# Two transformer blocks in one kernel: another order of the work at the borders between stages

## The chip, the cores and the metric

The kernel runs on one core of one Trainium2 chip. The time is the device time of one execution in microseconds; the number given for a kernel is the median of its runs. TensorE (PE in the profile) multiplies, VectorE (DVE) and ScalarE (ACT) do the elementwise work, GpSimd (POOL) makes constants, SyncE (SP) issues all DMAs.

## The reference

Everything is float32, on 256 tokens of width 2048. Two blocks follow each other.

```python
# first block, two layers
h = rmsnorm(x, norm_g[l]); proj = h @ w_in[l]            # 6 x conv, 4 groups of diff, 2 of mem
y_a = short_gated_conv(a_x, a_b, a_c, conv_w[l], conv_b[l]) * silu(a_g)
y_d = diff_attention(rmsnorm(q), rmsnorm(k), v, lam, slopes) (normed) * silu(d_g)   # 6 heads
mkv = rmsnorm(mem, mem_norm_g[l]) @ w_mem_kv[l]
y_m = memory_attention(rmsnorm(mq), rmsnorm(mk), mv) * silu(m_g)                    # 4 heads
x = x + concat(y_a, y_d, y_m) @ w_out[l]
# second block, one layer; mod = silu(c) @ w_mod + b_mod gives sh1, sc1, g1, sh2, sc2, g2
h = rms(x) * (1 + sc1) + sh1; proj = h @ w_in_2
o_a = sliding_window_attention(rope(q_a), rope(k_a), v_a, sinks)
o_b = rms(gla_chunked(q_b, k_b, v_b, gk), gla_norm) * silu(og_b)
merged = sigmoid(g_a) * (o_a @ w_br_a) + sigmoid(g_b) * (o_b @ w_br_b)
x = x + g1 * rms(merged @ w_out_2)
x = x + g2 * rms(conv_ffn(rms(x) * (1 + sc2) + sh2))
```

## The kernel before

**Precision and units.** Each product is computed from parts: an activation tile and a weight tile are each split into a high part (rounded to fp32r) and a low part (the rest). The activations stand in `XH[:, tile, 0:512]`, high in the first 256 columns and low in the others, for 16 tiles of the contraction. A *unit* is 512 KB of weights, four contraction tiles by two output tiles. It lands by DMA in one of five RAW buffers, ACT rounds it to `WH` (`act_split`, L540), DVE subtracts to get `WL` (`dve_split`, L549), and PE multiplies: `WH` with 512 columns (L468), `WL` with 256 (L473), 16 matmuls a unit. `WH` and `WL` are rings of four, so at unit w the engines split unit w+4 (`split_ahead`, L555), and ACT's split waits until PE is done with unit w. Semaphore `unit_done` counts PE's units, `split_ready` DVE's splits.

**Stages.** A stage is one matrix (mem0, mem1, qkv0, heads0a to heads0c, out0, and so on), its pairs of output tiles take `per_pair` units each, usually four. A turn is `body` pairs. After the units of a pair ACT copies the part of the bank that came from the low activations to `HIGH` (L804) and DVE adds the two and finishes (`evacuate`, L938 to L961). In token stages (v_b, out1, mix_out and the down stages) the tokens are on the partitions of the output and a pair is 512 output columns for both halves of the tokens; their unit, two contraction tiles by four output tiles, is 12 matmuls (L415 to L417).

**Order of the work.** All instruction streams are written out by hand and each engine runs its own in order. In `act_stage` and `dve_stage` a turn goes over b and q: the split for four units ahead, then whatever is attached to this place (squares, sums, attention steps `act_beside`, `dve_beside`, one step of the modulation product `dve_modulation`, L1932), then after the pair the evacuation. PE has attached work too, in `pe_stage`, and waits in order for what it needs. SP issues the loads of units and modulation steps in one order (`program_sync`); each waits until the buffer five loads back is used.

**Borders.** The next stage's input is split chunk by chunk, four tiles each (`act_input_chunk`, L1121 and L1127; `dve_input_chunk`, L1138 and L1146). `input_waits` (L1106) holds a chunk until its source is ready and until the old stage no longer reads those tiles of XH. `then` and `inside` (L239 to L247) say how many chunks are placed in the last pair of the old stage; the rest follow its last evacuation.

Around the change:

- mem0 to mem1: the four chunks of mem1's input are in mem0's last pair. In the same turn ACT squares x for its norm (`act_squares`, L1094, at w 3 and 4) and DVE adds them up (`dve_presum`, L1076 and L1078, at w 5 and 6); PE sums them over partitions in mem1 after unit 1 (`presummed_sums`, L1084).
- heads0c and heads1c (`beside="mem"`) carry two turns of memory attention: at w 2 scores, w 3 exps, w 5 transposes (L1247) and their copy by ACT (`act_copy_turned`, L1307), w 6 values (L1268), w 7 output. In turn 0 ACT also makes the Silu of the gates M_G (4 tiles) and D_G (6 tiles) at w 4 (L1411 to L1415). In the third turn the branches are finished: Silu of A_G, products, chunks 0 to 2. Chunk 3 follows the last evacuation (`act_mix_end`, `dve_mix_end`), then a table load.
- out0 ends with x1's chunks 0 to 2 inside and chunk 3 behind, branch_b with those of m.
- g_b's input is all 16 tiles of XH; branch_a's (oa) has 8 tiles, placed at 0 to 7; branch_b's (ob) has 16: chunks 0 and 1 in branch_a's last pair, 2 and 3 behind it.

## Time and profile before

| what | value |
|---|---|
| runs | 2597.15, 2598.98, 2601.71 us, median 2598.98 |
| profiled execution, span | 2596.0 us (its own device time is not given apart from the span) |
| PE busy | 98% |
| DVE busy | 75% |
| ACT busy | 50% |
| DMA | 556.64 MB, 214 GB/s |
| mean granted TensorE clock | 0.995 |

The span goes from the first to the last instruction. Units follow each other on PE at an even pace, so a border is read by its excess over whole units. PEclk in a window is the granted clock as a share of 2.4 GHz; 0.50 is 1.2 GHz. In a timeline the first number is the start, the second the time until the end of the group, and the bracket tells for how long the engine was idle before and what released it.

### The profile page before, as it was taken

Reading aid. Unit: us, or ns where it says so; the run is one execution under the profiler, and the core shown is the slowest. Engines: PE = TensorE matmul, PEld = TensorE weight load, DVE = VectorE, ACT = ScalarE, POOL = GpSimd, SP = SyncE. Lnnn points to the kernel's source line nnn. Section 1 sums busy time; section 2 is a strip of 40 time slices with the busy share of each in tenths; the row PEclk is TensorE's granted clock in tenths of the full one; section 3 lists DMA queues with packets and bytes.
Section 4 is the critical chain, followed back from the end, with each engine's and each line's share of the span. In section 5 each row is a group of like instructions: output and inputs, shape, how many; then the busy total and the mean of one; then the engine's idle time right before and its main releaser. Section 6 shows DMA issues by size and latency. Waiting matters only on the chain.

```text
span 2596.0 us, 35319 instructions
## 1 busy us (share of the span) xinstructions
PE 2547.3 (98%) x13936; PEld 2175.1 (84%) x13936; DVE 1939.5 (75%) x2769; ACT 1300.1 (50%) x1758; POOL 10.8 (0%) x62
## 2 busy tenths in 40 slices
PE   7999999999999999999999999999999999999998
PEld 6888888888888887888788888888888888888886
DVE  6877766887777687676667787887788887788855
ACT  7544555554455555454444554544644443444443
POOL 0000000000000010000000000000000000000000
PEclk9999999999999999999999999999999999999999
DMA  8687554778754466755567788888476668976764
GB/s 271 219 299 244 160 154 143 228 258 286 242 158 152 149 214 218 235 171 154 153 190 222 231 277 277 270 282 272 143 197 189 188 208 307 284 203 196 201 194 140
DMA packets 526519, 556.64 MB, mean 214 GB/s; under 512 B 17409, under 2 KB 453762, under 8 KB 526226
## 3 DMA queue, kind: packets, MB, share of 16 engines
q1 hardware_dynamic: 526354, 554.38, 68.4%
q8 instruction: 110, 1.80, 0.3%
q14 instruction: 55, 0.45, 0.1%
HBM read 552.22 MB, written 2.10 MB: 214 GB/s over the span
## 4 chain that ended last, share of the span: by engine, by line
PE 88%; DVE 7%; ACT 3%; issue 1%; DMA 0%; DVEq 0%; SPq 0%; ACTq 0%
PE ACC L468 43%; PE ACC L473 21%; PE ACC L415 6%; PE ACC L417 6%; PE ACC L416 6%; DVE WL L549 2%; PE OU L1268 1%; ACT WH L540 1%; PE SC L1235 1%; PE SC L1247 1%; ACT PROB L1293 1%; PE SC L1276 1%; DVE XH L1138 0%; DVE XH L1146 0%; DVE PROB L1352 0%
## 5 line engine op out<-in xcount | busy, mean ns | idle before, releaser
L468 PE MATMUL ACC<-XH,WH 128*128 128x512 f32 x5296 | 1692.3, 401 | 21.2 <-DVE XH L1146 15.3
L540 ACT ACTIVATE WH<-RAW 128x1024 fp32r<-128x1024 f32 (+1 forms) x852 | 897.9, 1057 | 1166.5 <-PE ACC L473 836.1
L549 DVE TENSOR_TENSOR WL<-RAW,WH 128x1024 fp32r<-128x1024 f32 (+1 forms) x852 | 1032.6, 1220 | 568.5 <-ACT WH L540 567.0
L473 PEld LDWEIGHTS ACC<-XH,WL 128*128 128x128 f32 x5296 | 998.7, 189 | 236.6
L473 PE MATMUL ACC<-XH,WL 128*128 128x256 f32 x5296 | 1044.2, 279 | 0.0
L468 PEld LDWEIGHTS ACC<-XH,WH 128*128 128x128 f32 x5296 | 814.4, 189 | 41.2 <-issue 18.5
L1932 DVE SCALAR_TENSOR_TENSOR RAWMOD<-RAWMOD,CSILU 128x1024 f32<-128x1024 f32 x192 | 233.8, 1218 | 1.0 <-DMA RAWMOD<-in_w_mod_t 0.7
L415 PE MATMUL ACC<-WH,XH 128*128 128x512 f32 x384 | 151.9, 396 | 3.6 <-DVE WL L549 3.6
L416 PE MATMUL ACC<-WL,XH 128*128 128x512 f32 x384 | 149.6, 390 | 0.0
L417 PE MATMUL ACC<-WH,XH 128*128 128x512 f32 x384 | 149.5, 389 | 0.0
L415 PE MATMUL ACC<-WH,AH 128*128 128x512 f32 x352 | 137.3, 390 | 0.0
L417 PE MATMUL ACC<-WH,AH 128*128 128x512 f32 x352 | 137.0, 389 | 0.0
L416 PE MATMUL ACC<-WL,AH 128*128 128x512 f32 x352 | 137.0, 389 | 0.0
L415 PEld LDWEIGHTS ACC<-WH,XH 128*128 128x128 f32 x384 | 72.1, 188 | 22.1 <-issue 7.5
L804 ACT ACTIVATE HIGH<-ACC 128x512 f32<-128x512 f32 (+1 forms) x171 | 89.9, 526 | 0.0
L417 PEld LDWEIGHTS ACC<-WH,XH 128*128 128x128 f32 x384 | 72.1, 188 | 15.3
L416 PEld LDWEIGHTS ACC<-WL,XH 128*128 128x128 f32 x384 | 72.1, 188 | 14.4
L417 PEld LDWEIGHTS ACC<-WH,AH 128*128 128x128 f32 x352 | 66.1, 188 | 13.8
L416 PEld LDWEIGHTS ACC<-WL,AH 128*128 128x128 f32 x352 | 66.1, 188 | 13.5
L415 PEld LDWEIGHTS ACC<-WH,AH 128*128 128x128 f32 x352 | 66.1, 188 | 13.5
L938 DVE TENSOR_TENSOR PR<-ACC,HIGH 128x512 f32<-128x512 f32 x64 | 43.7, 682 | 3.6 <-ACT HIGH L804 3.6
L979 DVE SCALAR_TENSOR_TENSOR CV<-U,PARAM,CV 128x256 f32<-128x256 f32 x88 | 42.7, 485 | 3.1
(287 smaller groups left out, 1438.0 us busy)
## 6 DMA issues: line engine op xcount, KB each, us to landing
RAW<-in_w_in SPq DMA_DIRECT2D x408, 512.0 KB, 4.5
RAWMOD<-in_w_mod_t SPq DMA_DIRECT2D x192, 512.0 KB, 4.9
RAW<-in_w_up SPq DMA_DIRECT2D x176, 512.0 KB, 4.7
RAW<-in_w_out SPq DMA_DIRECT2D x96, 512.0 KB, 5.4
RAW<-in_w_down SPq DMA_DIRECT2D x88, 512.0 KB, 5.0
RAW<-in_w_mem_kv SPq DMA_DIRECT2D x32, 512.0 KB, 5.8
RAW<-in_w_branch_gla SPq DMA_DIRECT2D x32, 512.0 KB, 5.1
RAW<-in_w_branch_attn SPq DMA_DIRECT2D x16, 512.0 KB, 5.2
```

The lines of the kernel that those rows point to most:

```text
L415: pe.matmul(bank, x, high[:, kc], start=tile == 0, stop=False)
L416: pe.matmul(bank, x, low[:, kc], start=False, stop=False)
L417: mm = pe.matmul(bank, operand[:, tile, T + b * P:T + b * P + P], high[:, kc], start=False, stop=tile == WK * stage.per_pair - 1)
L468: return pe.matmul(bank, k.WH[:, w % RING, kc, cols], x, start=tile == 0, stop=False)
L473: return pe.matmul(bank[:, 0:T], k.WL[:, w % RING, kc, cols], x[:, 0:T], start=False, stop=tile == tiles - 1)
L540: act.activation(k.WH[:, slot, :, 0:width], k.RAW[:, r % RAWS, :, 0:width], ACT.Copy).then_inc(k.hi_ready, 1)
L549: dve.tensor_tensor(k.WL[:, slot, :, 0:width], k.RAW[:, k.plan.unit_load[unit] % RAWS, :, 0:width], k.WH[:, slot, :, 0:width].bitcast(F32) ...
L804: act.activation(k.HIGH[:, first:stage.tiles], k.ACC[:, bank + first:bank + stage.tiles, T:2 * T], ACT.Copy).then_inc(k.high_ready, 1)
L938: chain.link(dve.tensor_tensor(dst, low, high, ALU.add))
L979: dve.scalar_tensor_tensor(out=cv, in0=u[:, 0:T], scalar=column(taps[0]), in1=cv, op0=ALU.mult, op1=ALU.add).then_inc(done, 1)
L1235: mm = pe.matmul(k.SC[:, c, b * T:b * T + T], q, keys, start=True, stop=True)
L1932: dve.scalar_tensor_tensor(out=raw, in0=raw, scalar=1.0, in1=k.CSILU[:, half * MOD_COLS:(half + 1) * MOD_COLS], op0=ALU.mult, op1=ALU.mult ...
```

## The change

1. `evacuates_first` for heads0c, heads1c, out0 and branch_b: in the last pair the split for four units ahead and the modulation step of the last unit stand behind the evacuation, on ACT and DVE.
2. In heads0c and heads1c, turn 0: Silu of M_G right after the copy of the turned probabilities at w 5, Silu of D_G and the table load at w 6.
3. The squares of x move from mem0's last turn (w 3, 4) to mem1's first (w 1, 2), their presums to w 2 and 3, PE's sums and ACT's rstd from after unit 1 to after unit 4 of mem1, the memory keys from 3 to 6, on DVE from 4 to 7.
4. Table loads ahead of out0, out1, mix_out and down1 are left out; loads of the same set stand later in out0 (w 6), mix_out and down1 (second pair, q 1).
5. g_b goes over its k tiles in the order 2, 3, 0, 1 (`MIXED`), with the rows of the weights to match; branch_a's input is placed in XH tiles 8 to 15 and read there; ob's chunks 0 and 1 go into tiles 0 to 7 inside branch_a (turns 1 and 2, w 1), chunks 2 and 3 into its last pair.

Left out below: the new attributes of `Stage` (`ahead`, `order`, `evacuates_first`) and the field `place` of `Prep` (0; for oa 2 * UK), which is added to f in both input chunk functions.

```diff
...
@@ -122,6 +123,13 @@
     view = w.rearrange("(k p) n -> p k n", p=P)
     return lambda j, q: view[:, UK * q:UK * q + UK, bass.ds(first + 2 * P * j, width)]
+
+
+def mixed_columns(w, first):
+
+    view = w.rearrange("(k p) n -> p k n", p=P)
+    return lambda j, q: view[:, UK * MIXED[q]:UK * MIXED[q] + UK,
+                             first + 2 * P * j:first + 2 * P * j + 2 * P]
@@ -215,7 +223,7 @@
     s.append(Stage("og", columns(w, 5648), 4, 8, 4, h2, "plain", OG, beside="gla", first=0))
     s.append(Stage("g_a", columns(w, 7696), 4, 8, 4, h2, "plain", G_A, beside="gla", first=2))
-    s.append(Stage("g_b", columns(w, 9744), 4, 8, 2, h2, "plain", G_B))
+    s.append(Stage("g_b", mixed_columns(w, 9744), 4, 8, 2, h2, "plain", G_B))
     oa_in = split_input(2)
     s.append(Stage("branch_a", columns(d["w_branch_attn_2"][0], 0), 2, 8, 2, oa_in, "times", G_A))
@@ -241,6 +249,10 @@
         by_name[name].then, by_name[name].inside = then, inside
     by_name["qkv1"].sums_last = 2
+    by_name["branch_a"].ahead = 2
+    by_name["g_b"].order, by_name["branch_a"].order = MIXED, MIXED
+    for name in ("heads0c", "heads1c", "out0", "branch_b"):
+        by_name[name].evacuates_first = True
     for l in range(DEPTH):
         by_name[f"heads{l}c"].inside = 3
@@ -459,6 +471,8 @@
         else:
             s, tile, tiles = h, UK * q + kc, UK * stage.per_pair
+            return (k.ACC[:, bank0 + s], operand[:, UK * stage.order[q] + kc], s, tile, tiles, kc,
+                    slice(h * P, h * P + P))
         return (k.ACC[:, bank0 + s], operand[:, tile], s, tile, tiles, kc,
                 slice(h * P, h * P + P))
@@ -505,11 +519,11 @@
                     for c in range(4):
                         presummed_sums(pe, k, 0, c)
-                if stage.name == "mem1" and (i, w) == (0, 1):
+                if stage.name == "mem1" and (i, w) == (0, 4):
                     pe.wait_ge(k.rstd_ready, 1)
                     for c in range(4):
                         presummed_sums(pe, k, 1, c)
-                if stage.name == "mem1" and (i, w) == (0, 3):
+                if stage.name == "mem1" and (i, w) == (0, 6):
                     pe_memory_keys(pe, k, 0)
                 if stage.name == "qkv0" and (i, w) == (0, 5):
@@ -552,6 +566,11 @@
 
 
+def at_end(stage, last, b, q):
+
+    return stage.evacuates_first and last and b == stage.body - 1 and q == stage.per_pair - 1
+
+
 def split_ahead(engine, k, stage, i, w, last, split):
@@ -572,6 +591,8 @@
             if stage.name == "out1" and (j, q) == (2, 5):
                 act_rotary(act, k)
+            if stage.name in ("mix_out", "down1") and (j, q) == (1, 1):
+                act.preload_act_table_set("natural_log_exp_and_others")
             if stage.name == "down1" and j == 0 and q in (2, 4, 6, 8):
                 act_gain_rows(act, k, 1, q // 2 - 1)
@@ -758,7 +779,8 @@
         for b in range(stage.body):
             for q in range(stage.per_pair):
-                split_ahead(act, k, stage, i, b * stage.per_pair + q, last, act_split)
+                if not at_end(stage, last, b, q):
+                    split_ahead(act, k, stage, i, b * stage.per_pair + q, last, act_split)
                 act_beside(act, k, stage, i, b * stage.per_pair + q, chain)
                 if stage.kind == "ffn":
@@ -774,13 +796,13 @@
                 if stage.name == "mem0" and (i, w) == (1, 2):
                     act_small(act, k)
-                if stage.name == "mem0" and i == 1 and w in (3, 4):
+                if stage.name == "mem1" and i == 0 and w in (1, 2):
                     act.wait_ge(k.x_landed, 64)
-                    for c in (2 * w - 6, 2 * w - 5):
+                    for c in (2 * w - 2, 2 * w - 1):
                         act_squares(act, k, 1, c)
-                if stage.name == "mem1" and (i, w) == (0, 1):
+                if stage.name == "mem1" and (i, w) == (0, 4):
                     act_rstd(act, k, 1, chain)
-                if stage.name == "mem1" and (i, w) == (0, 3):
+                if stage.name == "mem1" and (i, w) == (0, 6):
                     act_memory_keys(act, k, 0, chain)
                 if stage.sums_last is not None and w == 3 and i == 0:
@@ -794,8 +816,12 @@
                 if stage.name == "g_b" and w == 6:
                     act_gain_rows(act, k, 0, i)
+                if stage.name == "branch_a" and w == 1 and i in (1, 2):
+                    act_input_chunk(act, k, k.preps["ob"], i - 1)
+                if stage.name == "out0" and (i, w) == (0, 6):
+                    act.preload_act_table_set("natural_log_exp_and_others")
                 if last and b == stage.body - 1 and q < stage.inside and stage.then:
-                    act_input_chunk(act, k, k.preps[stage.then], q)
+                    act_input_chunk(act, k, k.preps[stage.then], q + stage.ahead)
             bank = 2 * ((stage.pair0 + b) % 2)
             first = 1 if stage.kind == "ffn" else 0
@@ -804,10 +830,12 @@
                            k.ACC[:, bank + first:bank + stage.tiles, T:2 * T],
                            ACT.Copy).then_inc(k.high_ready, 1)
+            if at_end(stage, last, b, stage.per_pair - 1):
+                split_ahead(act, k, stage, i, stage.units - 1, last, act_split)
 
     stage_turns(stage, turn)
     if stage.then is not None:
-        for c in range(stage.inside, k.preps[stage.then].chunks):
+        for c in range(stage.inside + stage.ahead, k.preps[stage.then].chunks):
             act_input_chunk(act, k, k.preps[stage.then], c)
     if stage.norm is not None:
@@ -1003,7 +1031,8 @@
             for q in range(stage.per_pair):
                 w = b * stage.per_pair + q
-                split_ahead(dve, k, stage, i, w, last, dve_split)
+                if not at_end(stage, last, b, q):
+                    split_ahead(dve, k, stage, i, w, last, dve_split)
                 if stage.kind == "ffn" and q == 2:
                     gate(i, b)
@@ -1014,26 +1043,36 @@
                     dve_modulation_sums(dve, k, k.plan.mod_adds[unit], chain)
                 dve_beside(dve, k, stage, i, w, chain)
-                if stage.name == "mem0" and (i == 0 and w in (1, 2) or i == 1 and w in (5, 6)):
-                    for c in (2 * (w - 4 * i) - 2, 2 * (w - 4 * i) - 1):
-                        dve_presum(dve, k, i, c, chain)
+                if stage.name == "mem0" and i == 0 and w in (1, 2):
+                    for c in (2 * w - 2, 2 * w - 1):
+                        dve_presum(dve, k, 0, c, chain)
+                if stage.name == "mem1" and i == 0 and w in (2, 3):
+                    for c in (2 * w - 4, 2 * w - 3):
+                        dve_presum(dve, k, 1, c, chain)
                 if stage.name == "mem0" and (i, w) == (0, 6):
                     dve_lambdas(dve, k, chain)
-                if stage.name == "mem1" and (i, w) == (0, 4):
+                if stage.name == "mem1" and (i, w) == (0, 7):
                     dve_memory_keys(dve, k, 0)
                 if stage.name == "qkv0" and (i, w) == (0, 6):
                 if stage.name == "kv_a":
                     dve_decays(dve, k, w)
-                for n in k.plan.mod_steps.get(unit, ()):
+                if not at_end(stage, last, b, q):
+                    for n in k.plan.mod_steps.get(unit, ()):
+                        dve_modulation(dve, k, n)
+                if stage.name == "branch_a" and w == 1 and i in (1, 2):
+                    dve_input_chunk(dve, k, k.preps["ob"], i - 1)
+                if last and b == stage.body - 1 and q < stage.inside and stage.then:
+                    dve_input_chunk(dve, k, k.preps[stage.then], q + stage.ahead)
+            evacuate(i, b)
+            if at_end(stage, last, b, stage.per_pair - 1):
+                split_ahead(dve, k, stage, i, stage.units - 1, last, dve_split)
+                for n in k.plan.mod_steps.get(end_unit(stage) - 1, ()):
                     dve_modulation(dve, k, n)
-                if last and b == stage.body - 1 and q < stage.inside and stage.then:
-                    dve_input_chunk(dve, k, k.preps[stage.then], q)
-            evacuate(i, b)
 
     stage_turns(stage, turn)
     if stage.then is not None:
-        for c in range(stage.inside, k.preps[stage.then].chunks):
+        for c in range(stage.inside + stage.ahead, k.preps[stage.then].chunks):
             dve_input_chunk(dve, k, k.preps[stage.then], c)
@@ -1108,15 +1147,20 @@
         wait_from_zero(engine, sem, value)
     if prep.free is not None:
-        early = prep.free.per_pair - c - 1 if c < prep.free.inside else 0
-        engine.wait_ge(k.unit_done, end_unit(prep.free) - early)
+        stage = prep.free
+        if c < stage.ahead:
+            engine.wait_ge(k.unit_done, stage.unit0)
+            return
+        inside = c - stage.ahead
+        early = stage.per_pair - inside - 1 if inside < stage.inside else 0
+        engine.wait_ge(k.unit_done, end_unit(stage) - early)
 
 
     input_waits(act, k, prep, c)
     if prep.gain is None:
-        f = 4 * c
+        f = 4 * c + prep.place
         for first, count in prep.chunk(c):
             last = act.activation(k.XH[:, f:f + count, 0:T], k.PR[:, first:first + count, :],
...
@@ -1204,7 +1249,7 @@
         "y1": prep(plan.y_in[1], "heads1c", mixed_ready(1), chunk=mixed),
         "oa": prep(plan.oa_in, "g_b", lambda k, c: [(k.unit_out, units_of(2) + 8)], chunks=2,
-                   chunk=tiles(O_A)),
+                   chunk=tiles(O_A), place=2 * UK),
         "ob": prep(plan.ob_in, "branch_a", lambda k, c: [(k.gated, 1)], chunk=tiles(V_B)),
         "m": prep(plan.m_in, "branch_b", pairs_of("branch_b"), chunk=tiles(G_A)),
@@ -1408,15 +1453,16 @@
     elif w == 1 and kind == "win" and stage.first + i == 0:
         act_decay_logs(act, k)
-    elif w == 4 and kind == "mem" and i == 0:
-        act.wait_ge(k.evacuated, stage.pair0)
-        act_silu(act, k, M_G, MEM_T)
-        act_silu(act, k, D_G, DIFF_T)
-        act.preload_act_table_set("natural_log_exp_and_others")
     elif w == (4 if kind == "win" else 3):
         act_exps(act, k, kind, u, sinks=2 * (stage.first + i) if kind == "win" else None)
     elif w == (6 if kind == "win" else 5):
         act_copy_turned(act, k, kind, u)
+        if kind == "mem" and i == 0:
+            act.wait_ge(k.evacuated, stage.pair0)
+            act_silu(act, k, M_G, MEM_T)
+    elif w == 6 and kind == "mem" and i == 0:
+        act_silu(act, k, D_G, DIFF_T)
+        act.preload_act_table_set("natural_log_exp_and_others")
     elif w == 6 and kind == "mem" and i == 1:
         act_conv_centre(act, k, stage.layer)
@@ -2125,7 +2171,6 @@
             products(name.format(l))
         act_mix_end(act, k, l)
-        tables()
         products(f"out{l}")
     act_token_norm(act, k, s["out1"], chain)
@@ -2137,12 +2182,10 @@
     products("branch_a")
     products("branch_b")
-    tables()
     products("mix_out")
     act_token_norm(act, k, s["mix_out"], chain)
     for name in ("up0", "down0", "up1"):
         products(name)
-    tables()
     products("down1")
```

## Rows read from the trace of the kernel before

**Rows 1.** the page, part 1: busy us of each engine, share of the span, instructions

```profile
PE 2547.3 (98%) x13936; PEld 2175.1 (84%) x13936; DVE 1939.5 (75%) x2769; ACT 1300.1 (50%) x1758; POOL 10.8 (0%) x62
```

**Rows 2.** PE's waits: engine line waited for: us in total, times, longest

```profile
PE OU L1268 <- ACT TURNED L1307: 4.5, 2, 2.3
```

**Rows 3.** windows: stretch, us, busy us (instructions) by engine, PEclk, DMA share, GB/s

```profile
650.83:664.77 13.94, 13.94 (x83) 12.16 (x82) 10.85 (x14) 6.27 (x7) 0.00 (x0) 1.00 0.83 260
950.62:972.38 21.76, 21.76 (x97) 18.02 (x96) 15.78 (x20) 10.62 (x13) 0.00 (x0) 1.00 0.90 298
57.02:72.39 15.37, 11.97 (x59) 10.01 (x57) 13.34 (x25) 12.90 (x24) 0.00 (x0) 0.89 0.30 105
27.43:31.76 4.33, 4.33 (x27) 3.79 (x25) 3.32 (x6) 1.06 (x1) 0.00 (x0) 1.00 1.10 347
409.72:421.31 11.59, 9.33 (x43) 7.69 (x42) 3.07 (x3) 6.16 (x6) 0.00 (x0) 0.85 0.45 137
441.97:449.36 7.39, 7.39 (x43) 6.47 (x42) 6.34 (x7) 5.46 (x9) 0.00 (x0) 1.00 0.54 156
477.23:481.97 4.74, 2.95 (x18) 2.39 (x16) 2.74 (x5) 3.13 (x5) 0.00 (x0) 1.00 0.38 121
936.72:942.38 5.66, 2.88 (x14) 2.10 (x12) 3.36 (x5) 4.90 (x6) 0.00 (x0) 1.00 0.16 61
569.78:581.13 11.35, 8.94 (x42) 7.55 (x41) 9.28 (x15) 6.28 (x9) 0.00 (x0) 0.85 0.58 186
1657.35:1665.36 8.01, 5.99 (x35) 4.91 (x33) 7.98 (x11) 7.47 (x9) 0.00 (x0) 1.00 0.82 272
1760.04:1763.71 3.67, 2.88 (x13) 2.10 (x12) 2.47 (x4) 3.66 (x4) 0.00 (x0) 1.00 0.24 88
```

**Rows 4.** timeline of ACT before out1: start us, us, engine line op tiles [idle before]

```profile
938.62 1.28 ACT L2115 ACT_TABLE_LOAD   x1
939.92 1.06 ACT L540 ACTIVATE WH<-RAW 128x1024 fp32r<-128x1024 f32 x1
```

**Rows 5.** timeline of ACT in mem0's last pair

```profile
52.89 2.00 ACT L1094 ACTIVATE PR<-X 128x1024 f32<-128x1024 f32 x2
```

**Rows 6.** timeline of DVE from mem0's last pair into mem1

```profile
53.01 1.23 DVE L549 TENSOR_TENSOR WL<-RAW,WH 128x1024 fp32r<-128x1024 f32 x1 [4.56 <-ACT WH L540]
...
62.56 0.69 DVE L1076 TENSOR_TENSOR PR<-PR 128x512 f32<-128x512 f32 x1
...
64.68 1.66 DVE L1146 SCALAR_TENSOR_TENSOR XH<-Y,PARAM,XH 128x256 fp32r<-128x256 f32 x4
...
66.26 1.22 DVE L549 TENSOR_TENSOR WL<-RAW,WH 128x1024 fp32r<-128x1024 f32 x1
...
73.83 0.68 DVE L938 TENSOR_TENSOR PR<-ACC,HIGH 128x512 f32<-128x512 f32 x1
...
76.67 2.35 DVE L549 TENSOR_TENSOR WL<-RAW,WH 128x1024 fp32r<-128x1024 f32 x2
...
78.94 1.22 DVE L1932 SCALAR_TENSOR_TENSOR RAWMOD<-RAWMOD,CSILU 128x1024 f32<-128x1024 f32 x1
```

**Rows 7.** timeline of DVE at the end of heads0c

```profile
476.61 0.68 DVE L938 TENSOR_TENSOR PR<-ACC,HIGH 128x512 f32<-128x512 f32 x1
...
477.33 0.69 DVE L940 TENSOR_TENSOR PR<-PR,RSTD 128x512 f32<-128x512 f32 x1
...
478.72 0.69 DVE L1577 TENSOR_TENSOR PR<-PR 128x512 f32<-128x512 f32 x1 [0.70 <-ACT PR L1508]
...
480.63 1.29 DVE L1138 TENSOR_TENSOR XH<-PR,XH 128x512 fp32r<-128x512 f32 x2 [1.22 <-ACT XH L1121]
```

**Rows 8.** timeline of DVE at the start of out1

```profile
941.01 2.36 DVE L549 TENSOR_TENSOR WL<-RAW,WH 128x1024 fp32r<-128x1024 f32 x2 [1.07 <-ACT WH L540]
```

**Rows 9.** timeline of DVE at the end of out0

```profile
570.23 0.69 DVE L950 TENSOR_TENSOR SUM<-ACC,HIGH 128x512 f32<-128x512 f32 x1
...
573.42 1.67 DVE L1146 SCALAR_TENSOR_TENSOR XH<-X,PARAM,XH 128x256 fp32r<-128x256 f32 x4 [1.77 <-ACT XH L1127]
```

12 lines of the change are left out of this document (7 added, 5 removed).

## The prediction

> **What bounds the kernel now.** I read the page first: TensorE (PE) is busy for 2547.3 of the 2596.0 us of the span [rows 1], so this change can give back only what PE waits. The list of PE's waits comes next, for what it waits for: of the waits touched here it names one pair, the value matmuls for ACT's copy into TURNED, 4.5 us in two times [rows 2]; the others are waits for DVE at stage borders. Then the windows. In an undisturbed stretch five units of 16 matmuls take 13.94 us, 2.79 us each, and eight units of a token stage take 21.76 us, 2.72 each [rows 3]. Against these two numbers every window at a border shows its loss directly; the reader should subtract whole units and look at PEclk, the granted clock. Where it is under 1.00, part of the window ran at 1.2 GHz instead of 2.4. Last, the timelines of DVE and ACT at the borders, to see what their queues hold.
>
> The losses that the edits touch, all from [rows 3]:
> - mem0 to mem1, 57.02 to 72.39: three units and the four sums. Three units are 8.36, the sums cost 4.33 - 2.79 = 1.54, so the loss is 15.37 - 9.90 = 5.47. It is two waits and a stretch at the low clock (0.89).
> - heads0c, 409.72 to 421.31: 11.59, where the same two units of the next turn take 7.39 at full clock: 4.20. It comes twice, once in each layer (two waits in [rows 2]): 8.4.
> - heads0c to out0: 4.74 - 2.79 = 1.95. heads1c to out1: 5.66 - 2.72 = 2.94.
> - out0 to qkv1, 569.78 to 581.13: 11.35 less two units (5.58) and sums (1.54): 4.23. The mean clock of 0.85 says that 0.15 x 11.35 = 1.7 of it is missing clock, the price of one fall; the wait is the other 2.5.
> - branch_a to branch_b: 8.01 - 5.58 = 2.43. branch_b to mix_out: 3.67 - 2.72 = 0.95.
>
> Together 26.4 us, about 1% of the time. No edit can bring more.
>
> **Silu of the memory gates.** Today ACT runs both Silus and two table loads between the exps and the copy of the turned probabilities, and PE's value matmuls wait for the copy [rows 2]. In the new order the copy comes right after PE's transposes, within the 2.79 us of the unit that PE runs in between. What moves behind it is a table load (1.28, [rows 4]), the Silu of M_G's four tiles, a split, the Silu of D_G's six and a second load: 1.0, 1.06 and 1.5 for the three in between, at 1.0 for each four tiles as in the squares [rows 5] and 1.06 for the split [rows 4], some 6 us in all. PE needs none of it: the only PE work behind ACT is a split used three units, 8.4 us, later, and DVE needs M_G after the value matmuls. Both losses should go with their low clock: **-8.4**. If that cover failed, PE would wait again at the same place for up to the same time; bounds 0 and -8.4. I take the full value, since the turn behind it, which has no Silu, shows 7.39 [rows 3].
>
> The table load takes 1.28 us in the trace, and ACT's next instruction starts 1.30 after it began [rows 4]. The Trainium skill (ScalarE: Activation LUTs, What ACT_TABLE_LOAD costs) adds a drain of about 1.38 us to each switch. By that the block would be 2.8 us longer, still inside the 8.4 us, so the sum would stay, while the chance of the second rival below would double.
>
> **mem0 to mem1.** The squares of x leave ACT ahead of the chunks of mem1's input: two groups of 2.00 [rows 5]. ACT then has chunk 0 ready about 3.8 us earlier, and every DVE low part comes before PE wants it. The loss of 5.47 goes. But the work comes back in mem1. PE now does the sums of x after unit 4 of mem1 and needs all four presums there. PE arrives at 57.02 + 6 x 2.79 = 73.75. DVE is in order and, from its split at 53.01 on (the row shows the idle 4.56 before it), has without a hole: nine splits at 1.135 (half of 78.94 - 76.67; 10.2), one evacuation (1.34, as two operations in [rows 7]), four input chunks at 1.58 (6.3), the block of the last evacuation, small gains and key squares (76.67 - 73.83 = 2.84), one modulation step (1.15), and two pairs of presums at 2.12 (4.24) [rows 6]. That is 26.1, so the last presum ends near 79.1. It stands behind split 7 of mem1, and PE, also in order, waits for it, 5.4 us nearly idle, with its units 5 and up queued behind the sums. Three quarters of the 1.54 for the sums pass in that time, so unit 5 starts at 79.65 instead of 75.29: 4.36 lost. In the trace such long waits were followed by half clock; with one fall at 1.7 that is **+6.1**. Net: -5.47 + 6.06 = **+0.6**. Bounds of the new wait: 0, if DVE were early, and 8.5, if the modulation step's transfer comes 2.5 late as well. I keep the queue's own sum since each term has a row. Behind PE's wait ACT's rstd waits too, and with it splits 9 on; these are needed three units later and PE is stopped anyway. The sums of the memory keys, two units later, wait for nothing new.
>
> **Evacuation ahead of the split.** At heads0c's end DVE's last evacuation starts one split (1.14) earlier than 476.61. Silu and the gate product follow, but the split now stands between evacuation and product: it ends 1.34 + 1.135 after the new start of 475.47, at 477.94, against 478.72 today. So 0.79 of the 1.14 stays, the low part of chunk 3 starts at 479.84 instead of 480.63 [rows 7], and PE too: **-0.8** of 1.95; 1.2 stay. Bounds 0 and -1.95.
>
> heads1c to out1 is the same chain (the same 0.8), but the wait is for the first split behind it, and the table load falls out: ACT's split comes 0.8 + 1.3 earlier, at 937.8. DVE is free for it only after chunk 3's low part, which today starts as the table load does: 938.62 - 0.8 + 1.3 = 939.1, against 941.0 today: **-1.9** of 2.94 [rows 3, 4, 8]. Bounds -0.8 and -2.9.
>
> At out0's end a split and a modulation step stand ahead of the evacuation, which starts at 570.23. It now goes first and they follow, all three ending at the old 571.57; chunk 3's high part is done on ACT by then, so the low part starts at 571.57, not 573.42 [rows 9]: -1.85, leaving a wait of 0.7. Waits of that size stand in the trace at full clock (0.95 at mix_out, [rows 3]), so the fall goes as well: **-3.55**. Bounds -1.1 and -4.2.
>
> branch_b to mix_out: the same edit with three evacuation steps, and a table load out of ACT's way. The first split behind the border comes over 2 us earlier, the wait was 0.95: **-0.95**. Here and at the other borders the last split (2 us later) frees its RAW buffer later, and SP's in-order queue holds the next loads; these have units to spare, since the first split that is late for PE today gets earlier. The moved preloads fall into ACT's idle time, nothing on PE's path.
>
> **Branches.** ob's chunks 0 and 1 are split inside branch_a into the half of XH that g_b has left, 2.1 us of ACT and 2.3 of DVE over two turns with slack. Chunks 2 and 3 are then where 0 and 1 were, wanted two units later: **-2.43**. g_b's other k order costs nothing: same bytes, same matmuls. Bounds -2.43 and +0.5 (a late split, if DVE's 7.98 busy of 8.01 at the border spread backwards).
>
> **Sum.** -8.4 + 0.6 - 0.8 - 1.9 - 3.55 - 0.95 - 2.43 = -17.4 us. The span of 2596.0 would be 2578.6. Of the profiled execution only its span is given; the median of the runs, 2598.98, lies 3.0 above it (2597.15 to 2601.71). With the same 3.0 around it: **2581.6 us**.
>
> **Rivals.**
> - *The presums are in time*: PE finds them, or DVE works ahead. For it: in the trace DVE does catch up within a turn. Against: no hole in its queue. Then 6.1 less: 2575.5. Chance 0.12.
> - *The Silu wait only changes its name*: DVE's output or a late split holds PE in the same unit. Against: 8.4 us of cover. Then +8.4: 2590.0. Chance 0.04.
> - *DVE's order gives nothing at the three borders with little slack* (out0, out1, qkv1), since the split that is put back takes what the evacuation gains; this is also the case that the change does not do there what it says. +0.8 + 1.9 + 1.85: 2586.2, or 2587.9 if the clock falls there too. For it: a third of the gain is lost so already at out0. Chance 0.12.
> - *Slower*: the long wait in mem1 brings the clock down and it stays down. Place: from 74 us on; price: the same 1.7 for each stretch like that after out0. It decides from 11 such stretches in a row (17.4 / 1.7 = 10.2); with 14 it is 2605.4. Against: after every wait of this trace the clock was back within one or two. Chance 0.03.
>
> **How the numbers follow.** My forecast has 0.63, its own range 2577.5 to 2585.5: one fall of the clock more or less at out1's end or in mem1 (1.7 each way) and 2 us for the border estimates. The rest, 0.06, is mixtures. The range 2574.5 to 2588.5 takes in the first and third rival and leaves out the others. A measurement here tells 0.2%, 5.2 us, from no change. Faster than 2593.8: 0.94; within: 0.04; slower: 0.02.
>
> **What would show it.** In the new trace: the value matmuls (L1268) out of PE's waits; no wait at the start of mem1, but one of about 5 us for DVE's presum at 74 us, with half clock behind it; waits of 1.2, 1.1 and 0.7 at out0, out1 and qkv1; none at branch_b and mix_out. I am wrong if the sums do not wait, if a border waits for a DMA, or if the clock falls at a wait of about 1 us.

## The result, and the profile after

The kernel after takes 2582.76 us (median of 4 runs, 2582.33 to 2582.91), beside 2600.35 us of the kernel before (4 runs, 2597.15 to 2602.24). The ratio is 0.9933, 95% interval 0.992 to 0.9947: 17.6 us less. The forecast was 2581.6, a step of -17.4. The span goes from 2596.0 to 2580.6 us. Repeated later beside 8 new runs of before (median 2598.73, 2596.86 to 2604.61), after took 2582.0 (5 runs, 2581.32 to 2583.65).

Page, part 1, of the kernel after: PE's busy time moves by only 3.6 us (2547.3 to 2543.7), with the same matmuls. The other 11.8 of the span's 15.4 are waiting.

```profile
PE 2543.7 (99%) x13936; PEld 2172.3 (84%) x13936; DVE 1939.0 (75%) x2769; ACT 1297.0 (50%) x1756; POOL 10.8 (0%) x62
```

PE's waits in the kernel after (waiting instruction, awaited instruction: us in total, times, longest). The value matmuls' wait for TURNED of [rows 2] is out of the list. L1117, the presum, is new, and so is L981, an evacuation in branch_a. The presum's 3.0 come in three pieces, since PE does each sum as soon as its presum is there.

```profile
PE OU L1123 <- DVE PR L1117: 3.0, 3, 1.5
...
PE ACC L482 <- DVE XH L1182: 1.0, 1, 1.0
PE ACC L482 <- DVE PR L981: 1.0, 2, 0.5
PE ACC L427 <- DVE WL L563: 0.8, 1, 0.8
```

Windows of the kernel after, from a unit's first matmul to another's (stretch, us, busy us of PE, PEld, DVE, ACT, POOL, PEclk, DMA share, GB/s). In order: mem0's last unit to mem1's third; mem1 units 4 and 5 with the sums; heads0c; out0's third unit; qkv1; heads1c; out1; kv_a's first three units; branch_a units 6 to 11; branch_a to branch_b; mix_out. They answer to the windows of [rows 3], except the second, the eighth and the ninth, which lie elsewhere.

```profile
56.43:64.79 8.36, 8.36 (x51) 7.29 (x49) 8.36 (x17) 8.06 (x16) 0.00 (x0) 1.00 0.61 191
70.36:84.08 13.72, 10.77 (x43) 8.04 (x41) 11.71 (x18) 3.87 (x6) 0.00 (x0) 0.75 0.77 231
410.11:417.48 7.37, 7.37 (x43) 6.46 (x41) 3.00 (x3) 7.32 (x7) 0.00 (x0) 1.00 0.53 148
473.40:477.36 3.96, 2.95 (x18) 2.39 (x16) 2.74 (x5) 2.85 (x5) 0.00 (x0) 1.00 0.44 145
565.20:573.12 7.92, 7.37 (x42) 6.27 (x41) 7.92 (x13) 5.23 (x8) 0.00 (x0) 1.00 0.64 201
858.64:866.02 7.38, 7.38 (x44) 6.47 (x43) 3.01 (x3) 7.33 (x7) 0.00 (x0) 1.00 0.51 147
924.54:928.25 3.71, 2.88 (x13) 2.09 (x12) 2.57 (x4) 3.71 (x5) 0.00 (x0) 1.00 0.46 141
1063.96:1077.71 13.75, 13.75 (x66) 11.40 (x65) 5.52 (x6) 3.93 (x5) 0.00 (x0) 0.88 0.78 251
1617.84:1636.01 18.17, 17.16 (x99) 14.63 (x97) 16.11 (x21) 12.03 (x14) 0.00 (x0) 1.00 0.83 269
1644.47:1652.83 8.36, 8.36 (x51) 7.29 (x49) 8.33 (x11) 6.40 (x7) 0.00 (x0) 1.00 0.85 280
1744.62:1747.34 2.72, 2.72 (x14) 2.25 (x12) 2.72 (x3) 1.06 (x1) 0.00 (x0) 1.00 0.87 296
```

Read them by subtracting whole units, as before. The first is three units and nothing else: the 5.47 are gone. The second is 13.72, where two units with the sums take 7.30 in an undisturbed place (4.33 and 2.97, from mem0): 6.42 lost. Both heads windows are at the 7.4 of a turn without Silu. Branch_a to branch_b is three clean units, but six units inside branch_a take 18.17 instead of 16.72 (6 x 2.79).

The whole ledger, from stage start to stage start, in us:

| place | forecast | after - before |
|---|---|---|
| heads0c and heads1c (Silu) | -8.4 | -4.21 - 4.18 = -8.39 |
| mem0 and mem1 | +0.6 | +0.35 |
| heads0c to out0 | -0.8 | -0.76 |
| heads1c to out1 | -1.9 | -1.89 |
| out0 to qkv1 | -3.55 | -3.42 |
| branch_b to mix_out | -0.95 | -1.07 |
| branch_a and branch_b | -2.43 | -0.30 - 0.69 = -0.99 |
| q_a, kv_a, up0 (no edit there) | 0 | -1.95 + 1.55 + 1.12 = +0.72 |
| span | -17.4 | -15.4 |

Of the +0.35, the windows account for +0.95 (-5.47 + 6.42). Another -0.56 is the very first unit of mem0, 4.63 instead of 5.19, which no edit touches. That first unit takes 4.3 to 5.3 in the fourteen profiles, so the +0.35 is good to about 1 us only. The last row but one is nearly all the clock's: after's profile has 3.4 us of half clock at q_a where before's has 6.8, and 3.4 us each in kv_a and at up0's start, where before's has none. In up0 there is also a small gain that was not forecast. Its units 4 and 5 take 2.88 to 2.91 each in all five profiles without edit 4 and 2.79 in all nine with it. Where up0 has no fall, it takes 270.46 to 270.48 without the edit and 270.17 with it, 0.3 less. How the moved loads bring that about was not traced.

### The profile page after: what moved, and what is told of

It is laid out like the page before. It is cut to its first block, busy times and chain, and to the rows that moved or that the text cites. A ratio compares the mean times of both kernels' runs of the same rounds, so it can differ in the third digit from the quotient of the medians.

```text
span 2580.6 us, 35317 instructions
## 1 busy us (share of the span) xinstructions
PE 2543.7 (99%) x13936; PEld 2172.3 (84%) x13936; DVE 1939.0 (75%) x2769; ACT 1297.0 (50%) x1756; POOL 10.8 (0%) x62
## 4 chain that ended last, share of the span: by engine, by line
PE 91%; DVE 6%; ACT 2%; issue 1%; DMA 0%; DVEq 0%; SPq 0%; ACTq 0%
PE ACC L482 44%; PE ACC L487 22%; PE ACC L427 6%; PE ACC L429 6%; PE ACC L428 6%; DVE WL L563 2%; PE OU L1313 1%; PE SC L1292 1%; ACT WH L554 1%; PE SC L1280 1%; PE SC L1321 1%; DVE XH L1190 1%; ACT PROB L1338 1%; DVE PROB L1368 0%; DVE MX L1371 0%
## 5 line engine op out<-in xcount | busy, mean ns | idle before, releaser
L427 PEld LDWEIGHTS ACC<-WH,AH 128*128 128x128 f32 x352 | 66.1, 188 | 13.5
L428 PEld LDWEIGHTS ACC<-WL,AH 128*128 128x128 f32 x352 | 66.1, 188 | 13.5
L1007 DVE SCALAR_TENSOR_TENSOR CV<-U,PARAM,CV 128x256 f32<-128x256 f32 x88 | 42.7, 485 | 3.1
L1005 DVE SCALAR_TENSOR_TENSOR CV<-U,PARAM,CV 128x256 f32<-128x256 f32 x88 | 42.7, 485 | 3.1
```

What stands on the lines that cost most here:

```text
L427: pe.matmul(bank, x, high[:, kc], start=tile == 0, stop=False)
L428: pe.matmul(bank, x, low[:, kc], start=False, stop=False)
L1005: chain.link(dve.scalar_tensor_tensor(out=cv, in0=u[:, 1:1 + T], scalar=column(taps[1]), in1=cv, op0=ALU.mult, op1=ALU.add))
L1007: dve.scalar_tensor_tensor(out=cv, in0=u[:, 0:T], scalar=column(taps[0]), in1=cv, op0=ALU.mult, op1=ALU.add).then_inc(done, 1)
```

## Experiments

**The parts alone.** Each of the first four kernels is the kernel before with some of the five edits, one run each; before took 2601.47 beside them. Single runs scatter too much for their times to be added up (the four differ from 2601.47 by -13.5, +0.3, -9.5 and -2.1, in all -24.9), so each is read by its stage times, beside those of the profile of before. The theory was that the parts add up, each worth its own row in the ledger; the rivals were the prediction's: that Silu's wait only changes its name, that the presums are in time, and that DVE's order gives nothing.

silu_only, edit 2:

```
-    elif w == 4 and kind == "mem" and i == 0:
-        act_silu(act, k, M_G, MEM_T)
-        act_silu(act, k, D_G, DIFF_T)
...
     elif w == (6 if kind == "win" else 5):
         act_copy_turned(act, k, kind, u)
+        if kind == "mem" and i == 0:
+            act_silu(act, k, M_G, MEM_T)
+    elif w == 6 and kind == "mem" and i == 0:
+        act_silu(act, k, D_G, DIFF_T)
```

> The kernel before with the Silu edit alone. My theory (the copy of the turned probabilities is what PE waits for, and nothing behind it is late): heads0c 78.3 us from its first unit to out0's instead of 82.4, heads1c the same, each with no wait of the value matmuls and no fall of the clock there; -8.4 us in all and nothing anywhere else. Rival (the gain in the changed kernel came with the earlier evacuation or another edit): heads0c and heads1c at 80 us or more.

2587.93 us. heads0c 82.35 to 78.12, heads1c 82.30 to 78.12: -8.41, after has -8.39. Windows of silu_only at heads0c and at qkv1:

```profile
409.78:417.16 7.38, 7.38 (x43) 6.47 (x42) 3.02 (x3) 7.33 (x7) 0.00 (x0) 1.00 0.51 150
565.64:575.46 9.82, 7.39 (x43) 6.29 (x41) 7.79 (x13) 5.50 (x8) 0.00 (x0) 1.00 0.54 171
```

The second row is a by-product that matters below: out0's end is untouched here and PE waits as long as before, but the clock stayed at 1.00, and the window is 9.82 where [rows 3] have 11.35 at 0.85. The same wait has a fall behind it in one profile and none in the other. So "nothing anywhere else" did not hold: the run gained 13.5, the edit's own places 8.4.

squares_only, edit 3:

```
-                if stage.name == "mem1" and (i, w) == (0, 1):
+                if stage.name == "mem1" and (i, w) == (0, 4):
                     pe.wait_ge(k.rstd_ready, 1)
                     for c in range(4):
                         presummed_sums(pe, k, 1, c)
...
-                if stage.name == "mem0" and i == 1 and w in (3, 4):
+                if stage.name == "mem1" and i == 0 and w in (1, 2):
                     act.wait_ge(k.x_landed, 64)
```

> The kernel before with the squares of x and what hangs on them moved, alone. My theory: the loss of 5.5 us at mem1's start goes and a wait for DVE's last presum of about 5 us comes after unit 4 of mem1, with half clock behind it; qkv0 starts 0.3 us later than before (114.5 us after the span's start instead of 114.2). Rival (the wait in mem1 belongs to another edit): qkv0 starts near 108.7.

2601.73 us. mem0 and mem1 together 103.62, before 103.12: +0.5. The wait after unit 4 is there, 12.77 where after has 13.72; its fall is half as long (0.87 of the clock against 0.75). Windows of squares_only, mem1 units 4 and 5, and heads1c, which the edit does not touch:

```profile
71.30:84.07 12.77, 9.81 (x43) 7.28 (x42) 11.72 (x18) 3.87 (x6) 0.00 (x0) 0.87 0.71 228
867.07:876.97 9.90, 7.64 (x43) 6.52 (x42) 3.08 (x3) 6.15 (x6) 0.00 (x0) 1.00 0.43 119
```

In heads1c the old wait for TURNED had no fall behind it this time: the stage took 80.64, before 82.30.

evac_only, edits 1 and 4 (the order and the table loads together):

```
+            if at_end(stage, last, b, stage.per_pair - 1):
+                split_ahead(dve, k, stage, i, stage.units - 1, last, dve_split)
+                for n in k.plan.mod_steps.get(end_unit(stage) - 1, ()):
+                    dve_modulation(dve, k, n)
...
-        tables()
         products(f"out{l}")
```

> The kernel before with the last evacuation ahead of the splits in the four stages and the table loads moved, alone. My theory: -0.8 us at out0's third unit, -1.9 at out1's fourth, -3.5 at qkv1's third (1.85 of it wait, the rest clock), -1.0 at mix_out's fourth: -7.2 in all. Rival (the split that is put back takes all that the evacuation gains): under -2 in all.

2591.96 us: out0 -0.75, qkv1 -3.40, out1 -1.88, mix_out -1.07. The two edits together are worth all that after shows at these borders. loads_back, below, takes edit 4 out again: out0, qkv1 and mix_out stay as they are in after, so their gain is the order's alone, while at out1 the load has 1.2 of the 1.9 and the order the other 0.7.

branch_only, edit 5:

```
+                if stage.name == "branch_a" and w == 1 and i in (1, 2):
+                    dve_input_chunk(dve, k, k.preps["ob"], i - 1)
                 if last and b == stage.body - 1 and q < stage.inside and stage.then:
-                    dve_input_chunk(dve, k, k.preps[stage.then], q)
+                    dve_input_chunk(dve, k, k.preps[stage.then], q + stage.ahead)
```

> The kernel before with the other k order of g_b, the place of branch_a's input and the two early chunks of branch_b's, alone. My theory after the changed kernel's trace: no wait at branch_b's start (-2.5), but two waits of 0.66 us in branch_a (+1.5), each for the evacuation (DVE) that stands behind an early chunk: -1.0 from g_b's start to mix_out's. Rival (the waits in branch_a come from the other phase that the other edits give the DMAs): no wait in branch_a and -2.5.

2599.37 us. branch_a -0.26, branch_b -0.69: -0.95, not -2.43. Window of branch_only, branch_a units 6 to 11:

```profile
1633.66:1651.85 18.19, 17.18 (x99) 14.63 (x97) 16.12 (x21) 12.02 (x14) 0.00 (x0) 1.00 0.83 273
```

It loses the same 1.5 as after, at full clock. The four kernels together give -8.41 + 0.50 - 7.10 - 0.95 = -15.96, after's own rows for the same places -8.39 + 0.35 - 7.14 - 0.99 = -16.17: the parts add up.

**Taking each new wait away.** The next kernels are the kernel after with one thing changed. sums_later moves the sums and rstd of x to after unit 6 of mem1, and the memory keys behind them:

```
-                if stage.name == "mem1" and (i, w) == (0, 4):
+                if stage.name == "mem1" and (i, w) == (0, 6):
                     pe.wait_ge(k.rstd_ready, 1)
                     for c in range(4):
                         presummed_sums(pe, k, 1, c)
```

> The changed kernel with PE's sums of x and ACT's rstd after unit 6 of mem1 instead of unit 4, and the memory keys one unit into the second turn. My theory (PE came to the sums 5 us before DVE's queue had them, and the low clock came from that wait): PE gets there at 78.7, the last presum ends at 78.6, no wait, no fall; mem1 takes 48.9 us instead of 55.3. Rival (DVE is short of time in mem1 and the wait moves on to the keys or to a split): mem1 at 52 us or more.

2575.94 us in one run, before 2602.45 beside it. mem1 takes 48.91 instead of 55.32: -6.41, as much as the window of after shows lost. Window of sums_later from unit 4 of mem1 to unit 9, five units with sums and keys:

```profile
70.62:88.78 18.16, 18.16 (x102) 15.18 (x101) 17.66 (x26) 8.59 (x11) 0.00 (x0) 1.00 0.78 243
```

PE is busy all of it. So nearly is DVE (17.66): its backlog is worked off behind PE's units instead of in front of them.

chunk_after puts ob's early chunk on DVE one unit later, behind the evacuation of the pair before:

```
-                if stage.name == "branch_a" and w == 1 and i in (1, 2):
+                if stage.name == "branch_a" and w == 2 and i in (1, 2):
                     dve_input_chunk(dve, k, k.preps["ob"], i - 1)
```

> The changed kernel with DVE's part of branch_b's early chunks behind the evacuation (w 2) instead of ahead of it (w 1), ACT's part where it was. My theory (the chunk's 1.14 us stands in front of an evacuation that had 0.5 us of slack; behind it 0.74 of idle absorbs most): no wait in branch_a, the stage takes 44.6 us instead of 46.1, branch_b stays at 89.2. Rival (DVE has no room for the two chunks in these turns wherever they stand): branch_a at 45.5 or more.

2579.65 us. branch_a 44.59 instead of 46.14, and its window, here of chunk_after, is six whole units:

```profile
1618.11:1634.83 16.72, 16.72 (x99) 14.59 (x98) 15.44 (x20) 11.61 (x13) 0.00 (x0) 1.00 0.87 272
```

The timeline of DVE in the kernel after shows what stood there: a modulation step and the chunk ahead of the evacuation at 1622.61 (start, us, instruction, in the bracket the idle time before it).

```profile
1619.19 1.23 DVE L563 TENSOR_TENSOR WL<-RAW,WH 128x1024 fp32r<-128x1024 f32 x1 [0.74 <-ACT WH L554]
1620.33 1.22 DVE L1978 SCALAR_TENSOR_TENSOR RAWMOD<-RAWMOD,CSILU 128x1024 f32<-128x1024 f32 x1
1621.48 0.08 DVE L1978 DVE_READ_ACCUMULATOR RAWMOD<-RAWMOD,CSILU 128x1 f32 x1
1621.48 1.22 DVE L1182 TENSOR_TENSOR XH<-PR,XH 128x1024 fp32r<-128x1024 f32 x1
1622.61 0.68 DVE L978 TENSOR_TENSOR SUM<-ACC,HIGH 128x512 f32<-128x512 f32 x1
1623.33 0.69 DVE L981 TENSOR_TENSOR PR<-PR,SUM 128x512 f32<-128x512 f32 x1
```

**What the clock costs in the long wait.** Two kernels keep after's wait for the presums and let PE work through part of it, with matmuls whose result is not used (nothing is left out). warm_wait:

```
                     pe.wait_ge(k.rstd_ready, 1)
+                    for n in range(40):
+                        pe.matmul(k.OU[:, 1, 0:P], k.IDENT[:, :], k.ONES[:, :], start=True,
+                                  stop=True)
                     for c in range(4):
```

> The changed kernel with 40 small matmuls without use (128x128, some 4.5 us) ahead of the sums of x, in the time in which PE waits for the presums. My theory (of the 6.4 us lost there 4.7 are wait and 1.7 the clock that falls because PE stands still): the wait is the same, no fall of the clock behind it, mem1 takes 53.6 us instead of 55.3. Rival (the slow matmuls after the wait have another cause): 55.3 or more.

2587.63 us, mem1 57.84: a miss. The group in PE's timeline of warm_wait says why:

```profile
73.64 9.09 PE L525 MATMUL OU<-ONES,IDENT 128*128 128x128 f32 x80
```

Each fp32 matmul is recorded as two passes of 0.11, so 40 of them take 9.09, longer than the wait they were to fill. What it does show: no fall in mem1, and the next unit takes 2.97, not 4.73. warm_short is the same with 20:

> The changed kernel with 20 matmuls without use ahead of the sums of x instead of 40. Each of the 40 ran as two passes of 0.11 us, so 40 took 9.1 us and hid the wait under themselves; 20 take 4.5, less than the wait of 4.7. My theory: no fall of the clock, unit 4 to unit 5 of mem1 as in the changed kernel (9.0 us, 0.3 at most more), unit 5 to 6 2.97 us instead of 4.73: mem1 53.6 to 53.9 us instead of 55.3. Rival (the slow matmuls behind the wait are not the clock's): 55.3 or more.

2581.02 us, mem1 53.37. Window of warm_short, units 4 and 5:

```profile
71.31:83.07 11.76, 11.76 (x82) 10.85 (x81) 11.59 (x17) 3.87 (x6) 0.00 (x0) 1.00 0.72 224
```

The 20 take 4.46, and with the sums they fill the wait to within 0.1: unit 4 with all of it takes 8.79 (after 8.99), and the last presum ends 8.28 after the start of unit 4 in both, with one sum of 0.39 behind it. At full clock unit 5 takes 2.97 instead of 4.73. So of the 6.42 of after 4.46 are left at full clock, and 1.96 were the clock's: 1.76 in unit 5 and 0.20 in the sums ahead of it. PE in the kernel after, where the clock went to 0.5 at 76.3, inside the wait, and stayed there for 6.8 us:

```profile
77.63 2.28 PE L1123 MATMUL OU<-PR,ONES 128*128 128x256 f32 x4 [1.50 <-DVE PR L1117]
```

**The table loads.** loads_back is after without edit 4, so that ACT loads a table ahead of out0, out1, mix_out and down1 again:

```
         act_mix_end(act, k, l)
+        tables()
         products(f"out{l}")
```

> The changed kernel with the table loads where they were (ahead of out0, out1, mix_out and down1) and the three moved ones left out. My theory (a load costs its 1.3 us and matters only where ACT's next split is awaited): out1 1.1 us longer (94.5 to 95.6), out0 and mix_out as they are. Rival after the Trainium skill (ScalarE: Activation LUTs, What ACT_TABLE_LOAD costs: 2.66 us with its drain): out1 2.4 us longer and mix_out 0.5 or more.

2589.81 us. out1 97.32 instead of 94.54, mix_out unchanged (98.10 beside 98.12). By the stage alone the +2.8 is nearer to the rival's 2.4 than to the 1.1 of the theory, so the windows have to tell them apart. Its span is 7.5 us over that of after. The other 4.7 lie elsewhere: q_a (+2.0) and kv_a (+1.6), where the half clock lasted twice as long as in after, and up0, mem0 and mem1 (+0.5, +0.5, +0.2). ACT's timeline and the windows of loads_back, out1's units 3 and 4 and mix_out's unit 3:

```profile
926.30 1.28 ACT L2157 ACT_TABLE_LOAD   x1
927.59 3.90 ACT L554 ACTIVATE WH<-RAW 128x1024 fp32r<-128x1024 f32 x4
```

```profile
925.16:934.47 9.31, 7.30 (x25) 5.56 (x24) 7.07 (x8) 6.30 (x7) 0.00 (x0) 0.82 0.49 148
1751.62:1754.34 2.72, 2.72 (x13) 2.25 (x12) 2.68 (x3) 1.91 (x2) 0.00 (x0) 1.00 0.90 282
```

At out1 the load is on the path: the unit with the wait grows from 3.71 to 4.89, by 1.2, about the 1.28 of the load. The rest of the 2.78 is a fall of the clock behind that wait (1.6), from 930.5 on, when that unit was over. At mix_out there was room for the load, and the rival's 0.5 did not come. The Trainium skill (ScalarE: Activation LUTs, What ACT_TABLE_LOAD costs) puts a drain of its own on each switch. Here the first instruction after the load starts 1.29 after it began, and the price on the path was 1.2, so the trace bears out the load alone.

**Both mended.** all_mended has sums_later, chunk_after, and at the borders of edit 1 the modulation step behind the rest of the input chunks as well:

```
                 split_ahead(dve, k, stage, i, stage.units - 1, last, dve_split)
-                for n in k.plan.mod_steps.get(end_unit(stage) - 1, ()):
-                    dve_modulation(dve, k, n)
...
             dve_input_chunk(dve, k, k.preps[stage.then], c)
+    if stage.evacuates_first:
+        for n in k.plan.mod_steps.get(end_unit(stage) - 1, ()):
+            dve_modulation(dve, k, n)
```

> The changed kernel with the sums of x after unit 6 of mem1, DVE's part of the early chunks behind the evacuation, and the last modulation step of a stage behind the following input's last chunk. My theory: -6.4 in mem1, -1.5 in branch_a, -0.7 at qkv1's third unit (the step's 1.15 us stood ahead of chunk 3's low part): 2574 us, 8.6 below the changed kernel, 2 either way for the clock's falls. Rival (what is gained at one wait is lost at the next, or the later memory keys hold qkv0): over 2578.

2575.18 us (4 runs, 2572.68 to 2577.03), ratio to before 0.9906 (0.9891 to 0.992), with the 2598.73 of the eight runs of before. mem1 48.91 and branch_a 44.59 as alone. Of the 0.8 left at qkv1 only 0.4 went (117.53 to 117.12), where 0.7 was expected. Window at qkv1, and the rows of ACT and DVE behind the evacuation, all_mended:

```profile
559.23:566.75 7.52, 7.39 (x43) 6.29 (x41) 6.88 (x12) 5.23 (x8) 0.00 (x0) 1.00 0.55 160
```

```profile
558.84 1.71 ACT L1172 ACTIVATE XH<-X,PARAM 128x256 fp32r<-128x256 f32 x4 [3.38 <-DVE X L989]
560.59 1.67 DVE L1191 SCALAR_TENSOR_TENSOR XH<-X,PARAM,XH 128x256 fp32r<-128x256 f32 x4 [0.64 <-ACT XH L1172]
```

Without the modulation step DVE comes early and waits 0.64 for ACT's high part of the chunk, all four tiles of it. ACT in turn was idle for 3.38 and began as soon as DVE's evacuation (L989) ended. So no queue holds the border any more, but the chain itself: evacuation, high part, low part.

after_again is the kernel after once more, to have it beside the mended ones:

> The changed kernel again, as the measure for the two next ones on the same chip: 2580 to 2584 us, with falls of the clock that come at other places than in its first trace.

2582.0 us (5 runs), ratio 0.9934 (0.9921 to 0.9947). The mends are worth 2582.0 - 2575.2 = 6.8 us. That the falls would come at other places did not hold: the second profile has them at the same four, in mem1, at q_a, in kv_a and at up0's start, and as long (6.8, 3.4, 3.4, 3.4). Its mem0 and mem1 together take 104.49, which is +1.37 over before and not +0.35.

mended_warm adds 13 unused matmuls on PE between out1's end and q_a, where all_mended has its longest wait behind the start (2.9 us, for the token norm) and its only fall of the clock before PE's last matmul. The wait in all_mended:

```profile
PE SC L747 <- DVE PR L939: 4.2, 2, 2.9
```

The edit:

```
+    pe.wait_ge(k.evacuated, s["q_a"].pair0 - 1)
+    for n in range(13):
+        pe.matmul(k.ACC[:, 2 * (s["q_a"].pair0 % 2), 0:P], k.IDENT[:, :], k.ONES[:, :],
+                  start=True, stop=True)
```

> The same with 13 matmuls without use (2.9 us) while PE waits for the normed tokens between out1 and q_a. My theory (the clock falls there since PE stands still for 3 us): no fall at q_a, which takes 46 us from its first unit instead of 47.5 (one fall) or 49 (two), so 1.5 to 3 us less than the mended kernel, and the wait itself stays (8.2 us from out1's last unit to q_a's first). Rival (the clock falls for another reason): same time, and a fall within 10 us of q_a's start.

2572.0 us (4 runs, 2571.86 to 2572.36), ratio 0.9894 (0.9879 to 0.991): the fastest version, 10 us below after. Windows from out1's last unit into q_a, of all_mended and then of mended_warm with its kv_a:

```profile
996.29:1017.71 21.42, 18.00 (x93) 15.35 (x92) 17.06 (x39) 14.14 (x28) 0.00 (x0) 0.84 0.39 129
```

```profile
995.55:1014.72 19.17, 18.22 (x119) 16.08 (x118) 16.44 (x39) 14.05 (x28) 0.00 (x0) 1.00 0.43 142
1056.52:1070.25 13.73, 13.73 (x66) 11.44 (x65) 5.20 (x6) 3.45 (x4) 0.00 (x0) 0.88 0.79 250
```

The 2.25 are clock only (0.84 to 1.00). q_a takes 47.17, without any fall, where 46 was expected. In place of the fall at q_a there came one in kv_a, 1.5 us. The four runs lie within 0.5 us of each other, the eight of before within 7.8.

## Why the prediction was right, and where not

The median moved by -17.6 with -17.4 forecast, but the profile's own time moved by -15.4. The difference lies in the frame: each run's time is 1.7 us above its span (2582.33 beside 2580.6, and so in every single run), so the 3.0 that the prediction laid around the span held 1.3 of scatter, and the second median of before stood 1.4 higher than the first. The span was forecast 2.0 too low, the time 1.2. That the two steps agree within 0.2 is luck: the branches gave 1.4 less, the clock elsewhere took 0.7, and the median gave 2.2 back, since the runs of before scatter and their second median lies 2.6 above the 2597.7 (2596.0 + 1.7) that belong to its profile.

- **Silu: right in place and size.** -8.39 for -8.4, and silu_only has it alone. Part of the size is the clock's: with no fall behind the old wait heads1c took 80.64 (squares_only), and the gain there would have been 2.5 instead of 4.2. Of the four profiles with the old order (before, squares_only, evac_only, branch_only) all have that fall in heads0c and three in heads1c. The cover it rested on is in ACT's timeline of after: the copy at 410.54, then load, Silus, a split and load until 417.55, the next split 0.19 after it, released by PE. The block took 6.0 for the 6.1 that its terms add up to. The side remark on the drain has a slip: 6.1 and 2.8 are 8.9, which is not inside the 8.4. The trace shows no drain, so nothing came of it.

```profile
410.54 1.01 ACT L1352 ACTIVATE TURNED<-SC 128x1024 f32<-128x1024 f32 x1
411.57 1.28 ACT L1554 ACT_TABLE_LOAD   x1
412.86 1.06 ACT L1554 ACTIVATE PR<-PR 128x1024 f32<-128x1024 f32 x1
413.83 1.04 ACT L554 ACTIVATE WH<-RAW 128x1024 fp32r<-128x1024 f32 x1
414.77 1.48 ACT L1554 ACTIVATE PR<-PR 128x1536 f32<-128x1536 f32 x1
416.27 1.28 ACT L1465 ACT_TABLE_LOAD   x1
417.74 1.06 ACT L554 ACTIVATE WH<-RAW 128x1024 fp32r<-128x1024 f32 x1 [0.19 <-PE ACC L487]
```

- **mem0 to mem1: right.** The 5.47 went and 6.42 came for 6.06 forecast. Over the five profiles that have this wait (after, after_again, squares_only, chunk_after, loads_back) it is 5.5 to 6.8, and the difference lies in where the half clock falls. DVE's in-order queue, summed from single rows of before, put the last presum at 79.1. It came at 78.64, from units that started 0.6 us earlier (56.43 instead of 57.02). DVE in the kernel after, at the end of that queue:

```profile
76.44 0.68 DVE L1115 TENSOR_TENSOR PR<-PR 128x512 f32<-128x512 f32 x1
77.15 0.42 DVE L1117 TENSOR_TENSOR PR<-PR 128x256 f32<-128x256 f32 x1
77.50 0.68 DVE L1115 TENSOR_TENSOR PR<-PR 128x512 f32<-128x512 f32 x1
78.21 0.43 DVE L1117 TENSOR_TENSOR PR<-PR 128x256 f32<-128x256 f32 x1
78.56 0.68 DVE L966 TENSOR_TENSOR PR<-ACC,HIGH 128x512 f32<-128x512 f32 x1
```

  It has no hole, as the prediction said against its first rival (presums in time), which is refuted. The one fall at 1.7 cost 1.96 (warm_short). That is near partly by luck: the half clock lasted 6.8 us, of which the first 3 lay in the wait and the sums, while in squares_only it lasted 3.4 and unit 5 took 3.77, only 0.8 more than at full clock. Two steps of this term were loose. From a last presum at 79.1 with one sum behind it unit 5 starts at 79.5, not 79.65, so the wait's share is 4.2 and not 4.36. And long waits were not always followed by half clock in the trace of before: out1's 2.94 stands in [rows 3] at 1.00.
- **Borders: right.** -0.76, -1.89, -3.42, -1.07 for -0.8, -1.9, -3.55, -0.95. The waits that stay are 1.2, 1.0 and 0.8 for 1.2, 1.1 and 0.7. The fall at qkv1 was counted as part of the gain. That holds for the one profile it was read from; silu_only has the long wait without it (squares_only and branch_only have the fall), so the order alone is sure of 1.9 and the other 1.5 depend on the run. The third rival (the order gives nothing) is refuted by evac_only with loads_back: out0 0.75, out1 0.7, qkv1 1.9 or more.
- **Branches: the step that failed.** -2.43 was forecast, -0.99 came. The border itself gave its 2.4: the window is 8.36, three clean units. What failed is "over two turns with slack". The turns had DVE time to spare, which is a sum over the turn, but not at unit 1: the chunk's 1.14 stands ahead of an evacuation that PE waits for, and its end had only about 0.4 to spare in both turns (an estimate, 1.14 less half of the 1.55 lost). That gives two waits (L981, 1.0 together), 1.55 in stage time, all of it gone in chunk_after, where the same work stands one unit later. The prediction's own bound of +0.5 had the direction ("a late split") with another place.
- **Slower by a clock that stays down** did not happen. In mem1 it was at 0.5 for 6.8 us, from inside the long wait on, and then back.
- **Not forecast:** +0.72 at q_a, kv_a and up0, where no edit is: about +1.0 from the clock, less the 0.3 in up0. These falls differ between the profiles of kernels that have the same code there (q_a 47.5 to 49.7, kv_a 26.1 to 29.3, up0 270.2 to 272.0), but the two profiles of after agree, so whether a kernel's own order settles part of it is open. The prediction's claim that the clock would keep up at waits of about 1 us held at all three borders that had one.

The forecast of mended_warm at q_a (46) was 1.2 too low: q_a without any fall is 47.17. The stretch from out1's last unit to q_a's first stayed at 8.2 us, and only the clock came back.

Left open: why the same wait is followed by a fall in one run and not in the other; and whether the 0.4 still lost at qkv1 can be had. Nothing stands ahead of ACT's high part there (it was idle for 3.38), so another order on ACT would not do it; letting DVE follow tile by tile instead of by the whole chunk was not tried.

## What to carry to other kernels

In kernels of in-order queues with a bound engine at 98%, price a moved step by the queue it lands in: list the instructions of the helping engine from its last idle time to the step, add single durations, and compare with when the bound engine arrives. Do this at the place itself; free time over a whole turn says nothing about a 1.14 us piece put ahead of an evacuation that has 0.4 us to spare. When something is in the way, move it one or two units, as both mends did here for 8.0 us of stage time (6.41 and 1.55), before looking for more parallelism.
